# Attention over cached value pages: two page steps in one TensorE event instead of one

## What is computed

```python
v_past = cache_v[l][page_table].reshape(b_s, past_len, N_ATTN_HEADS, HEAD_DIM)
p = jax.nn.softmax(s.reshape(b, H, qc, -1), axis=-1).reshape(s.shape)
return jnp.einsum('bhqkj,bhqkjd->bhqd', p, vs.astype(f32))
```

## Time and profile before

| | |
|---|---|
| median of 3 runs | 1788.47 us (1785.48 to 1790.24) |
| span of the profiled execution | 1787.6 us |
| TensorE busy (PE) | 1762.0 us, 99% of the span |
| VectorE busy (DVE) | 1194.6 us, 67% |
| ScalarE busy (ACT) | 912.3 us, 51% |
| loads of value pages | 64 of 512 KB, median 6.0 us from issue to landing |

### The profile page before, as it was taken

The page is one execution under the profiler, slowest core; times in us unless marked ns, Lnnn a source line. Parts: engine busy times, 40 slices in busy tenths (PEclk is TensorE's granted clock), DMA queues, the critical chain, the costliest instruction groups (busy, mean ns, idle before and its releaser), DMA issues.

```text
span 1787.6 us, 35222 instructions
## 1 busy us (share of the span) xinstructions
PE 1762.0 (99%) x14526; PEld 1712.9 (96%) x14526; DVE 1194.6 (67%) x1679; ACT 912.3 (51%) x1724; POOL 215.6 (12%) x127
## 2 busy tenths in 40 slices
PE   8999999999999999999999999999999999999997
PEld 8999999999998989889999999999999999999997
DVE  6468998999887656744754666666666666444444
ACT  5544556555676656633454655454554554434442
POOL 2145644554000000000000000000000000000000
PEclk8999999999999999999999999999999999999999
DMA  8589987888689999696575487777777776655553
GB/s 250 171 273 330 311 277 260 279 284 272 207 251 352 291 303 323 220 308 208 174 233 166 135 282 222 236 224 223 228 233 221 222 237 196 223 177 185 163 182 98
DMA packets 398273, 421.39 MB, mean 236 GB/s; under 512 B 13041, under 2 KB 375985, under 8 KB 397073
## 3 DMA queue, kind: packets, MB, share of 16 engines
q10 hardware_dynamic: 284480, 285.62, 50.1%
q1 hardware_dynamic: 113280, 132.85, 22.9%
q0 software_dynamic: 352, 0.67, 0.2%
HBM read 400.70 MB, written 18.66 MB: 235 GB/s over the span
## 4 chain that ended last, share of the span: by engine, by line
PE 87%; DVE 8%; ACT 2%; DMA 1%; issue 1%; SPq 0%; ACTq 0%; DVEq 0%; POOL 0%; POOLq 0%
PE gemm L1770 28%; PE gemm L1771 27%; PE gemm L1772 27%; DVE w_lo L1204 3%; PE side L2027 2%; PE side L1732 1%; DVE sc_flat L1401 1%; ACT w_hi L774 1%; DVE conv_out L1196 1%; DMA kv<-in_cache_v 1%; DVE u L1196 1%; DMA xtok<-in_x_prompt 0%; DVE un L1524 0%; PE side L1923 0%; DVE y L1196 0%
## 5 line engine op out<-in xcount | busy, mean ns | idle before, releaser
L1204 DVE TENSOR_TENSOR w_lo<-raw,w_hi 128x1024 fp32r<-128x1024 f32 (+1 forms) x562 | 732.2, 1306 | 547.1 <-ACT w_hi L774 546.0
L1770 PE MATMUL gemm<-x_hi,w_hi 128*128 128x264 f32 x3312 | 953.7, 288 | 5.7 <-DVE w_lo L1204 3.7
L1771 PE MATMUL gemm<-x_lo,w_hi 128*128 128x264 f32 x3312 | 938.7, 283 | 0.0
L1772 PE MATMUL gemm<-x_hi,w_lo 128*128 128x264 f32 x3312 | 938.6, 283 | 0.0
L774 ACT ACTIVATE w_hi<-raw 128x1024 fp32r<-128x1024 f32 (+1 forms) x562 | 585.7, 1045 | 660.6 <-PE gemm L1772 659.9
L1770 PEld LDWEIGHTS gemm<-x_hi,w_hi 128*128 128x128 f32 x3312 | 624.3, 189 | 34.3 <-issue 27.5
L1771 PEld LDWEIGHTS gemm<-x_lo,w_hi 128*128 128x128 f32 x3312 | 625.1, 189 | 0.8 <-issue 0.5
L1772 PEld LDWEIGHTS gemm<-x_hi,w_lo 128*128 128x128 f32 x3312 | 621.8, 188 | 0.0
L1771 PE MATMUL gemm<-g_lo,w_hi 128*128 128x264 f32 x704 | 200.4, 285 | 0.0
L1770 PE MATMUL gemm<-g_hi,w_hi 128*128 128x264 f32 x704 | 199.9, 284 | 0.0
L1772 PE MATMUL gemm<-g_hi,w_lo 128*128 128x264 f32 x704 | 199.6, 284 | 0.0
(11 more groups left out here) (324 smaller groups left out, 1403.9 us busy)
## 6 DMA issues: line engine op xcount, KB each, us to landing
raw<-in_w_in ACTq DMA_DIRECT2D x99, 1024.0 KB, 7.0
raw<-in_w_gate ACTq DMA_DIRECT2D x44, 1024.0 KB, 5.6
raw<-in_w_up ACTq DMA_DIRECT2D x44, 1024.0 KB, 5.2
raw<-in_w_down ACTq DMA_DIRECT2D x40, 1024.0 KB, 5.5
kv<-in_cache_k SPq DMA_DIRECT2D x64, 512.0 KB, 5.6
kv<-in_cache_v SPq DMA_DIRECT2D x64, 512.0 KB, 6.0
st<-in_state_ssm SPq DMA_DIRECT2D x64, 256.0 KB, 5.6
raw<-in_w_ssm_out ACTq DMA_DIRECT2D x16, 1024.0 KB, 6.6
```

The lines of the kernel that those rows point to most:

```text
L1204: v.tensor_tensor(w_lo[:, s, 0:blk.kts, cols], raw[:, s, 0:blk.kts, cols], w_hi[:, b % RING, 0:blk.kts].bitcast(fp32), ALU.subtract).then_ ...
L1770: mm(out, w_hi[:, b % RING, k], pr.hi[:, x], start=(x == 0), stop=False)
L1771: mm(out, w_hi[:, b % RING, k], pr.lo[:, x], start=False, stop=False)
L1772: ins = mm(out, w_lo[:, s, k, cols], pr.hi[:, x], start=False, stop=(x == pr.kt - 1))
```

## The change

The 32 events become 16, four to a group, five blocks apart (VG, VG+5, VG+10, VG+15 instead of VG, VG+2, ... VG+14). Event v of a group multiplies pages 2k and 2k+1 (k = v mod 4), all four slots at once: first the two pages in slots 0 and 1, then, behind a wait for `kv_in[1]`, the two in slots 2 and 3. The loads of slots 0 and 1 are issued 4 blocks before the event, those of slots 2 and 3 are issued 3 blocks before it, all of them after the event before (`v_mm`). The group's end moves by one block on VectorE (VG+18 to VG+19, VG+21 to VG+22) and on TensorE (VG+17 to VG+18).

```diff
--- before.py
+++ after.py
@@ -336,7 +336,7 @@
         STATE = [130 + 9 * m // 4 for m in range(4 * NB)]
         FS = [B_FF + 12 + 5 * m for m in range(4 * NB)]
         K_AT = [30 + int(K_PACE * m) for m in range(NB * NPG)]
-        V_AT = [VG[w] + 2 * g for w in range(4) for g in range(NPG)]
+        V_AT = [VG[w] + 5 * k for w in range(4) for k in range(4)]
 
         names = (
             "hi_done lo_done mm_done rows_in vecs_in pages_in state_in cs_out consts_made cst_t rows_cp "
@@ -495,18 +495,19 @@
 
             def value_loads(b):
 
-                for m in range(4 * NPG):
-                    if b != V_AT[m] - 4:
-                        continue
-                    w, g = m // NPG, m % NPG
-                    if m == 0:
-                        sp.wait_ge(k_red, NB * NPG)
-                    wait(sp, v_mm, m - 1)
-                    if g < 2:
-                        wait(sp, vs_mm, w)
-                    for e in range(2):
-                        src = vc[bass.ds(page_of(2 * w + e, g), 1)].rearrange("g p n -> p (g n)")
-                        sp.dma_start(page_slot(2 * m + e), src).then_inc(kv_in[m % 2], 16)
+                for v in range(16):
+                    w, k = v // 4, v % 4
+                    for half in range(2):
+                        if b != V_AT[v] - 4 + half:
+                            continue
+                        if v == 0 and half == 0:
+                            sp.wait_ge(k_red, NB * NPG)
+                        wait(sp, v_mm, v)
+                        if k == 0:
+                            wait(sp, vs_mm, w)
+                        for e in range(2):
+                            src = vc[bass.ds(page_of(2 * w + e, 2 * k + half), 1)].rearrange("g p n -> p (g n)")
+                            sp.dma_start(page_slot(2 * half + e), src).then_inc(kv_in[half], 16)
 
             hs = a["state_ssm"][0].rearrange("b h p n -> b (h p) n")
             ho = o["ssm_sample"][0].rearrange("b h p n -> b (h p) n")
@@ -1455,11 +1456,11 @@
             def values(b):
 
                 for w in range(4):
-                    if b == VG[w] + 18:
-                        dve.wait_ge(v_mm, NPG * (w + 1))
+                    if b == VG[w] + 19:
+                        dve.wait_ge(v_mm, 4 * (w + 1))
                         own = hmask[:, :].unsqueeze(2).to_broadcast([P, 8, HD])
                         mul(by_head(kv[:, 2, 0:512]), by_head(side[3][:, :]), own).then_inc(vm_done, 1)
-                    if b == VG[w] + 21:
+                    if b == VG[w] + 22:
                         dve.wait_ge(vs_mm, w + 1)
                         for h in range(2):
                             bs = slice(2 * w, 2 * w + 2)
@@ -2013,23 +2014,25 @@
 
             def values(b):
 
-                for m in range(4 * NPG):
+                for m in range(16):
                     if b != V_AT[m]:
                         continue
-                    w, g = m // NPG, m % NPG
-                    if g == 0:
+                    w, k = m // 4, m % 4
+                    if k == 0:
                         pe.wait_ge(own_done, 1)
                         wait(pe, v_cp, w)
-                    pe.wait_ge(kv_in[m % 2], 256 + 32 * (m // 2 + 1))
-                    for n in range(4):
-                        e, half = n % 2, n // 2
-                        first_col = (g * NB + 2 * w + e) * HEADS
-                        ins = mm(side[3][32 * n:32 * n + 32, :], sc_flat[:, first_col:first_col + 32],
-                                 page_slot(2 * m + e)[:, half * 512:(half + 1) * 512],
-                                 start=(g == 0), stop=(g == NPG - 1), skip_group_check=True)
+                    for half in range(2):
+                        g = 2 * k + half
+                        pe.wait_ge(kv_in[half], 256 + 32 * (m + 1))
+                        for n in range(4):
+                            e, part = n % 2, n // 2
+                            first_col = (g * NB + 2 * w + e) * HEADS
+                            ins = mm(side[3][32 * n:32 * n + 32, :], sc_flat[:, first_col:first_col + 32],
+                                     page_slot(2 * half + e)[:, part * 512:(part + 1) * 512],
+                                     start=(g == 0), stop=(g == NPG - 1), skip_group_check=True)
                     ins.then_inc(v_mm, 1)
                 for w in range(4):
-                    if b == VG[w] + 17:
+                    if b == VG[w] + 18:
                         pe.wait_ge(vm_done, w + 1)
                         for k in range(4):
                             ins = mm(side[3][:, 4 * k:4 * k + 4], kv[:, 2, k * P:(k + 1) * P], bsel[:, :],
```

## The result

The changed kernel took 1803.93 us (median of 4 runs, 1800.44 to 1808.98), beside 1788.17 (1785.48 to 1790.24) for the kernel before: ratio 1.0088, 95% interval 1.0071 to 1.0106. It is slower by 15.8 us in the medians, where I had forecast 4.6. The profiled execution was the fastest of the four: span 1798.7 against 1787.6, so it shows 11.1 us of the loss.

The account below looks back on a forecast made before the run. The prediction took TensorE as the bound nearly everywhere; -5.0 + 5.6 + 2.4 + 1.6, with -0.3 and +0.3, made +4.6 us, so 1793 us against 1788.5, called no change, with a range of 1787 to 1798.

Parts of the forecast that it names:

- Term 1: Value events on TensorE: 16 double events, each 0.31 us less than two single ones, give -5.0 us.
- Rival C: Halves of a double event don't stream, entry and exit are paid twice, no event gain: 1798 us, chance 7%.
- Term 2: First double event, block 152: TensorE waits for the second half's pages, +5.6 us, between 4.8 and 6.3.
- Term 3: First events of groups two and three: second-half pages come late, 1.5 and 0.9 us, together +2.4 us.
- "no wait" inside a group: Later events of a group: the second half has 4 blocks or 11.6 us from its issue, so no wait.
- Term 4: TensorE's clock falls to 1.2 GHz in block 152's wait: +1.6 us, between nothing and 4.6.
- Term 5: Block 210: TensorE arrives 2.1 us earlier, its operand `x_lo` 1.8, so +0.3 us more waiting.
- rival B: Waits for second halves decide: longer low clock, or 3 us each in groups two and three; 1796.5 us, chance 27%.

Follow-up runs that it names:

- e3_gate: The changed kernel with only the `gate_s` reload issued two blocks later, behind the pages of block 201: 1799.96 us, ratio 1.0056 to the kernel before.
- e5_warm: The changed kernel, no load moved, with TensorE repeating the first step's matmuls in each group's first event: 1797.49 us, ratio 1.0046 to the kernel before.
- e1_first: The changed kernel with only the four pages of block 152 loaded sooner, at SyncE's blocks 143 and 145: 1794.03 us, ratio 1.0026 to the kernel before.
- e2_slots: The changed kernel with the loads opening groups two to four issued sooner, slots 0 and 1 without waiting for `vs_mm`: 1793.90 us, ratio 1.0030 to before.

## Why the prediction was right and wrong

Right were the direction (the slow side), the mechanism and its first place; the size was a third of what came. By the prediction's own steps:

**Term 1, held.** -5.3 for -5.0; a further wave costs 0.43 us, where the earlier trace rows gave 0.44, and 5.3 lies between the 5.0 taken and the bound of 5.4. Rival C falls.

**Term 2, held.** 6.1 us for 5.6, within 4.8 to 6.3. The pages landed at 532.87, 7.3 us behind the event's start at 525.55; the forecast had them 6.5 us behind it (534.0 for 527.55).

**Term 3 failed.** "The same at the start of groups two and three: +2.4" was +5.6 (3.56 for 1.5, 2.02 for 0.9), and in the other profile 8.1 (4.79 and 3.32). I let SyncE issue without delay and counted only bytes. In group two the `crows` issue in front took 2.64 us where the median is 0.51 (3.43 in the other profile), so half 1 went out at 610.02 instead of 607.9: that is all of the 2.1 us missing there. The second of its pages, issued at 611.16, took 8.6 us more to land, where the median page takes 5.7. In group three `crows` took its usual 0.50 us; from the first page's issue to the last one's landing my sum had 12.8 us (681.9 to 694.7) and the trace has 13.9 (691.10 to 704.97), which is the missing 1.1. Why the loads took longer than their bytes there stays open.

**The same term's "no wait" inside a group failed.** The step was "the second half has 4 blocks or 11.6 us from its issue, as a page has today". The trace shows 8.9 us from issue (714.18) to need (723.1): half 1 goes out in block V-3, not V-4, and behind the eight `gate_s` loads of its block. It landed at 725.15. The kernel before also loads pages behind `gate_s`, but with 13.5 us to the event that wants them (702.18 to 715.70):

```profile
697.60 3.83 SPq L573 DMA_DIRECT2D gate_s<-gs_row  x8
702.18 16.85 SPq L509 DMA_DIRECT2D kv<-in_cache_v  x6
```
I listed the loads of the groups' starts and not those of the blocks between; the prediction itself named waits between events 2 to 4 as what would prove it wrong. e3_gate shows it by itself: 2.08 us to none.

**Term 4 failed in its count.** It priced one fall at 1.6; each cost more (1.8 and 2.6), and there were two, three in the other profile. The price was tied to term 2 alone, though term 3's waits stop TensorE as well. e5_warm shows that the idleness is the cause.

**Term 5, held.** The wait for `x_lo` at block 210 is 1.58 for 1.25.

**Sum.** Terms 2 to 4 were to be 9.6 and are 13.8 + 4.4 = 18.2 in the profiled execution. That is rival B, "the waits for the second half decide", past its point of 10.4. But B was priced as if only one of its two conditions could come true (7.6 to 8.2). Both did, nearly to their bounds: 4.4 us of clock for 4.6, and 5.6 of waits in groups two and three for 6. A wait I saw no cause for, 2.1 us, came on top. The range ended at 1798 for that reason. A second reason is that the sum was made for one execution: the changed kernel's time varies (1798.74 to 1809.28), and its first profile had 1.6 us less of page waits and one fall of the clock less than the other. The range's lower end was a slip too: no clock fall, groups two and three in time and a first wait of 4.8 give 1788.3 by the terms, not 1787.

## What to carry to other kernels

When a change makes one event need twice the inputs, count not bytes but places in the issuing queue: list every load between the first input's issue and the last one's, those of other stages too, and allow for issues that take longer than their median when several loads are in flight. Group the loads of one event together and ahead of loads that have time; here one block's move took the ratio from 1.0079 to 0.9979. Price each wait of TensorE with what its clock costs behind it, and price the places together, since they share a cause and come true together.

## What the runs showed of the hardware

- An issue instruction on SyncE isn't of fixed length. The 32 `crows` issues of the changed kernel have a median of 0.51 us, but five took 1.74 to 2.64 (1.98 at 522.95, 2.31 at 529.03, 2.64 at 606.57). All five had five to seven of SyncE's loads issued and not landed; with one or two in flight none took over 0.52 in this profile. That count doesn't decide it alone, since three with five in flight took 0.50 or 0.51, nor does a full DMA: its share was 1.11 at 522.95 but 0.70 at 606.57.
- The granted clock fell to 1.2 GHz behind every page wait of 2.30 us or more (2.30 in e1_first, 2.90 in e2_slots, up to 6.28 in e3_gate). Of the shorter ones it fell behind that of 1.92 (e5_warm) and not behind those of 1.97 (e3_gate), 2.02 and 2.08: the length of the wait doesn't decide it alone. Each time it stayed low for 3.4 or 6.8 us, most of it after dense work had begun again. Falls of 3.4 us cost 1.7 to 1.8 us each, those of 6.8 cost 1.8 to 2.9, by the times of the blocks behind them. The five falls of 3.4 us behind page waits came 0.5 to 1.5 us after TensorE had resumed, so a wait's cost isn't over with it.
- Filling the wait with repeats of the same matmuls kept 2.4 GHz and did not make the kernel slower: a way to keep the clock where the wait itself can't be moved.
